# More products that nobody reads, in eight places of a two-model transformer kernel

## What is computed

```python
def gated_deltanet(qkv, z, b_f, b_b, a_f, a_b, conv_w, A_log, dt_bias, norm_w):
    qkv = jax.nn.silu(depthwise_conv(qkv, conv_w))
    q, k, v = jnp.split(qkv, 3, axis=-1)
    q = l2norm(q.reshape(B, S, H, D))
    k = l2norm(k.reshape(B, S, H, D))
    ...
    g_f = log_decay(a_f, A_log[0], dt_bias[0])
    ...
    o_f = chunk_gated_delta(q, k, v, g_f, beta_f)
    o_b = rev(chunk_gated_delta(rev(q), rev(k), rev(v), rev(g_b), rev(beta_b)))
    o = rms_norm(o_f + o_b, norm_w) * jax.nn.silu(z.astype(f32).reshape(B, S, H, D))
```

## Time and profile before

| what | us |
|---|---|
| median of 3 runs | 4105.63 |
| lowest and highest | 4096.89, 4117.29 |
| the profiled execution | 4111.55 |
| its span in the trace | 4109.4 |
| TensorE busy in the span | 3790.7 (92%) |
| VectorE busy | 1583.6 (39%) |
| ScalarE busy | 1292.1 (31%) |
| mean granted clock of TensorE | 0.936 |

### The profile page before, as it was taken

One profiled execution on the slowest core, in us unless ns is written; L12 is line 12 of the kernel. 1 busy time (PEld: TensorE's weight loads), 2 busy tenths in 40 slices (PEclk: granted clock), 3 DMA queues, 4 the chain that ended last, 5 costly groups with the idle time before them and its releaser, 6 DMA issues. The chain is left out here.

```text
span 4109.4 us, 53438 instructions
## 1 busy us (share of the span) xinstructions
PE 3790.7 (92%) x20879; PEld 3207.1 (78%) x20879; DVE 1583.6 (39%) x2735; ACT 1292.1 (31%) x2313; POOL 420.9 (10%) x295
## 2 busy tenths in 40 slices
PE   8999998999999999899997898999999869999998
PEld 7777876787767787678775776777776649999997
DVE  3575534332456553433346544333435430000001
ACT  3474534231347453423133323222313311111111
POOL 0351002001135100200110001000000000000000
PEclk9988989999998898999998999999999889999999
DMA  4000011222200001222220002222220025666663
GB/s 143 35 1 1 0 61 65 95 86 82 90 26 1 1 0 52 72 92 92 82 85 24 1 22 81 80 97 80 100 97 28 21 105 204 230 221 217 224 233 132
DMA packets 64066, 344.96 MB, mean 84 GB/s; under 512 B 9116, under 2 KB 15132, under 8 KB 33452
## 3 DMA queue, kind: packets, MB, share of 16 engines
q1 hardware_dynamic: 59020, 330.65, 22.5%
q0 software_dynamic: 4896, 12.27, 1.5%
HBM read 328.33 MB, written 13.50 MB: 83 GB/s over the span
## 5 line engine op out<-in xcount | busy, mean ns | idle before, releaser
L562 PE MATMUL bank<-high 128*128 128x512 f32 x2384 | 941.6, 395 | 65.3 <-DVE low L689 31.8
L563 PE MATMUL bank<-low,high 128*128 128x512 f32 x2384 | 938.1, 394 | 0.0
L564 PE MATMUL bank<-high,low 128*128 128x512 f32 x2384 | 937.7, 393 | 0.0
L562 PEld LDWEIGHTS bank<-high 128*128 128x128 f32 x2384 | 454.3, 191 | 168.5 <-DVE low L689 36.2
L564 PEld LDWEIGHTS bank<-high,low 128*128 128x128 f32 x2384 | 453.7, 190 | 95.9
L563 PEld LDWEIGHTS bank<-low,high 128*128 128x128 f32 x2384 | 454.3, 191 | 95.2 <-issue 0.5
L610 ACT ACTIVATE high<-weight_ring 128x2048 fp32r<-128x2048 f32 (+1 forms) x151 | 280.3, 1858 | 715.9 <-PE bank L564 624.2
L689 DVE TENSOR_TENSOR low<-weight_ring,high 128x2048 fp32r<-128x2048 f32 (+1 forms) x151 | 338.6, 2244 | 237.2 <-ACT high L610 237.1
L3647 PE MATMUL bank<-chosen,glu_ring 128*128 128x176 f32 x2816 | 426.8, 314 | 2.7 <-ACT chosen L3711 2.7
L3647 PEld LDWEIGHTS bank<-chosen,glu_ring 128*128 128x128 f32 x2816 | 422.8, 191 | 4.7 <-issue 4.7
L239 PE MATMUL bank<-filler 128*128 128x512 f32 x709 | 240.2, 473 | 50.8 <-PEq L172 44.2
(11 more groups left out here) (555 smaller groups left out, 4695.1 us busy)
## 6 DMA issues: line engine op xcount, KB each, us to landing
glu_ring<-in_w_expert SPq DMA_DIRECT2D x88, 1024.0 KB, 6.9
weight_ring<-in_w_ff SPq DMA_DIRECT2D x64, 1024.0 KB, 4.9
down_ring<-in_w_expert_down SPq DMA_DIRECT2D x64, 704.0 KB, 5.0
weight_ring<-in_w_in SPq DMA_DIRECT2D x22, 1024.0 KB, 4.7
weight_ring<-in_w_ffe SPq DMA_DIRECT2D x22, 1024.0 KB, 4.9
weight_ring<-in_w_downe SPq DMA_DIRECT2D x16, 704.0 KB, 4.0
weight_ring<-in_w_ino SPq DMA_DIRECT2D x11, 1024.0 KB, 4.9
weight_ring<-in_w_ine SPq DMA_DIRECT2D x9, 1024.0 KB, 4.8
```

The costliest lines, as they stand in the source:

```text
L562: nc.tensor.matmul(mem.bank[b][:, :], whole, high[:, k, :], start=(k == 0), stop=False)
L563: nc.tensor.matmul(mem.bank[b][:, :], whole, low[:, k, :], start=False, stop=False)
L564: last = nc.tensor.matmul(mem.bank[b][:, :], rest, high[:, k, :], start=False, stop=(k == kt - 1))
```

## The change

Eight calls are touched. Seven get a higher count (6 to 12, 14 to 26, 14 to 26, 14 to 36, 4 to 7, 24 to 46, 52 to 54), and one call of 7 is new, at the head of TensorE's list in `delta_prepare`, ahead of its wait for the staged keys.

```diff
@@ mixer_norms
             last.then_inc(summed, 1)
-            fill_in(nc, mem, spread_banks[0], 6)
+            fill_in(nc, mem, spread_banks[0], 12)
...
                 last.then_inc(spread, 1)
-            fill_in(nc, mem, sums, 14)
+            fill_in(nc, mem, sums, 26)
@@ delta_inputs
         def _(pe):
-            fill_in(nc, mem, mem.bank[5], 14)
+            fill_in(nc, mem, mem.bank[5], 26)
             pe.wait_ge(g_ready, 1)
@@ delta_prepare
         def _(pe):
+            fill_in(nc, mem, mem.bank[0], 7)
             pe.wait_ge(staged, 1)
...
                     last.then_inc(turned, 1)
-            fill_in(nc, mem, mem.bank[0], 14)
+            fill_in(nc, mem, mem.bank[0], 36)
@@ delta_scan
                 last.then_inc(solved, 1)
-            fill_in(nc, mem, mem.bank[4], 4)
+            fill_in(nc, mem, mem.bank[4], 7)
             pe.wait_ge(solved_taken, 4)
@@ spatial_gate
             pe.wait_ge(taken, 3 * RW_PAIRS)
-            fill_in(nc, mem, gate_banks[0], 24)
+            fill_in(nc, mem, gate_banks[0], 46)
@@ compress
                     last.then_inc(outer, 1)
-            fill_in(nc, mem, turn_banks[0], 52)
+            fill_in(nc, mem, turn_banks[0], 54)
```

## The result

The changed kernel takes 4158.9 us (median of 4 runs, 4148.9 to 4168.1), the kernel before 4108.6 (4 runs): ratio 1.0131, 95% interval 1.0104 to 1.0158. It is slower by 1.3%, 54 us by the ratio, where I had forecast 30. The profiled execution took 4168.08 us, 56.6 more in its span than that of before.

The account below looks back on a forecast made before the run. TensorE, 92% busy, was taken to set the time, though fillers stand in waits for other engines. Terms 17.6 + 8.2 + 2.0 + 2.4 - 0.5 + 0.5 = 30.2 us on 4105.6 gave 4136 us; own range 4121 to 4150, outer 4108 to 4160.

Parts of the forecast that it names:

- Term 1: Preparation, six times: the added fillers outlast VectorE and lengthen the phase, +17.6 us, ends 6.6 and 39.6.
- four passes early and two late: Preparation: clock rises about 1 us after the seven fillers (1.1 us a pass), or only on the long filler run (6.6).
- The rule that was weighed: Preparation: sustained activity releases the slow clock; as it stands, all six passes would be early, 6.6 us.
- Step 4: Scan, six times: seven fillers make the next product 0.4 us late, 2.4 us in all.
- Term 2: Norms, twice: fillers ahead delay the products, trailing 26 outlast VectorE; 4.1 us each, 8.2 us in all.
- Terms 3, 5, 6: Inputs +2.0 us (each between +2.7 and -1.7); gate -0.5 us (ends 0.3 and -3); compression at most 0.5 us.
- the three parts named for "slower": Chances of over 4126 us: most of the forecast's part 0.43, the all-late rival 0.17, the all-early rival 0.04.
- rival B: Preparation: all six passes late, 52.2 us more, so 4158 us; chance 0.17.
- C: Inputs: fillers carry the 2.4 GHz clock through the 2-column sums, halving their low clock; not slower, 4112 us; chance 0.08.
- D: Whole change: trailing fillers don't hold the phase, as no semaphore waits for them; 4105 to 4112 us; chance 0.05.

Follow-up runs that it names:

- after_again: The changed kernel run once more, unaltered, for a second trace: 4155.9 us.
- rest_only: The kernel before with all the edits but the preparation's two: 4122.1 us, ratio 1.005.
- before_again: The kernel before run once more, unaltered, for a second trace: 4112.6 us.

## Why the prediction was right or wrong

**Sign and first mechanism: right.** Fillers outlast VectorE and hold the phase. Term 1, 17.6 us with four passes early and two late, was 16.4 with just these (19.2 in after_again). Over the five traces of kernels with 7 and 36, 2 of 30 passes kept their old length, 11 were early (17.4 to 17.6 us) and 17 late (22.1 to 23.3): "four of six" was luck in one trace; a little over half of the passes are late.

**The rule that was weighed.** The Trainium skill (TensorE: Matmul & The Clock Gate, What's actually happening) has sustained activity release the slow clock. The measurement decides against it as it stands, for a TensorE that is merely busy. Windows of after, an early pass and then a late one:

```profile
309.30:322.20 12.90, 12.87 (x74) 10.40 (x72) 11.71 (x40) 4.42 (x8) 5.04 (x4) 1.00 0.00 0
486.80:500.40 13.60, 13.60 (x52) 10.84 (x51) 13.60 (x49) 5.63 (x11) 4.98 (x4) 0.50 0.00 0
```

TensorE is busy all the time in both, at 1.00 in one and at 0.50 in the other.

**Step 4, the scan: wrong.** It reads "nothing follows but the chain of the scan: 6 x 0.4 = 2.4 us". The 0.4 is near (0.56: the fifth scan takes 26.89 in rest_only against 26.33, both without a fall), so of this step 3.4 us are the fillers. But the step looked behind the fillers only, took the products ahead of them as fixed, and treated the clock as a matter of the edited place. Measured 22.4, and 17.2 of these are the same 64 products, which spend more time at 1.2 GHz. The trace of before had the hint: of its first three scans two had a clock of 0.80 and one 1.00, so the same code had two prices, 1.6 us apart. That such a term existed could be read there, not its size: with all six scans at the dearer price the sum would have been 3.2 us longer.

**Term 2, norms**: 6.2 for 8.2. The overrun is 2.8 us each, as worked out; ahead of it the four products of the mean (L1463) ran partly at 2.4 GHz, 2.9 us instead of 3.8, which no term had. In rest_only the norms took 31.2 and 31.4 us in all, against 31.45 in the first trace of before and 27.4 in before_again, so this term too has a spread by the clock: it is 6.2 us between the first traces and 14.4 between the second. **Terms 3, 5, 6** lie inside their ends in the first traces: inputs +0.7 (+4.4 between the second), gate hidden with 0.1 us to spare, the stretch behind it 16.1 us for 17.5 (17.1 for 16.4 in the second, where a gain was forecast).

**The rest.** The 10.9 us in all the other stages belong to no place of the change that I could show, apart from 0.5 in the compression: the same remainder is 14.1 us longer in before_again than in the first trace of before, and 14.0 shorter in after_again than in the first of after. In the mean of the two traces of each kernel it does not grow (3473 us before, 3470 after), and the touched stages alone have the loss: preparations 17.9 us, scans 22.4, norms 10.3, inputs 2.6, together 53.1, against 54 by the ratio.

**The forecast as a whole.** 4158.9 lies beyond the forecast's own range of 4121 to 4150, and inside the outer one, to 4160, only because rival B had been given room. In the chances, the three parts named for "slower" add up to 0.64, not 0.63.

**Rivals.** B gave 4158, the measured time, for a cause that was not there (all six late). C fell: the 2-column sums still lost the clock (10.2 and 3.4 us at 0.50, as in the earlier trace rows). D fell in every preparation.

## What to carry to other kernels

A filler is free only while another engine ends later, and its length doubles where the clock is low: count it at the clock that the trace shows there, not at 2.4 GHz. An edit that changes the length of a phase also redraws the clock of untouched phases behind it; before pricing it, look whether equal stages in one trace have different times, because their spread shows that there is such a term. It does not bound it: 1.6 us a scan in the trace of before, 6.3 us over all the traces. A few fillers in the idle time just ahead of sparse products (here three, under another engine's last 0.7 us) kept the clock through those products in all 30 cases, where fillers behind them do nothing for them.

## What was not expected of the hardware

The clock falls during the scan's 64-column products for 0, 3.4, 6.8, 10.2 or 13.7 us, all with the same code in that stretch, and a fall 1.10 us after the first product lasted 10.2 us where one at 1.12 us lasted 3.4. A busy TensorE did not by itself raise the clock: the preparation's products (64 rows in the main) ran 9.1 us at 1.2 GHz, and in the norms of before, products with 2 columns ran from 555.12 to 568.77, 13.6 us, at 1.2 GHz throughout.
